# Two transformer blocks with a mixture of experts: token rows and gated products stored plainly and picked by TensorE with a stride, accumulators zeroed by GpSimd

## What is computed

```python
# per layer l, tokens t [512 in layer 0, 256 in layer 1, 1024]
g = softmax(t @ w_group + b_group); group = argmax(g)       # 4 groups of 8
e = logits inside that group; top 2 experts, shares by softmax
y[token] = sum over its 2 experts of share * ((silu(t @ w1[e]) * (t @ w3[e])) @ w2[e])
x = x + gate * y                                            # w1, w3: 1024x512, w2: 512x1024
```

## Time and profile before

| | |
|---|---|
| Median of 3 runs | 2652.04 us (2651.12 to 2653.01) |
| Profiled execution | 2647.32 us, its span 2645.5 us |
| TensorE products busy | 91% of the span |
| TensorE weight loads busy | 48% |
| VectorE, ScalarE, GpSimd busy | 32%, 15%, 3% |
| Experts of layer 0 | about 464 to 970 us of the span |
| Experts of layer 1 | about 1281 to 1760 us |

### The profile page before, as it was taken

One profiled execution on the slowest core, in us unless ns is written; L12 is line 12 of the kernel. 1 busy time (PEld: TensorE's weight loads), 2 busy tenths in 40 slices (PEclk: granted clock), 3 DMA queues, 4 the chain that ended last, 5 costly groups with the idle time before them and its releaser, 6 DMA issues.

```text
span 2645.5 us, 27917 instructions
## 1 busy us (share of the span) xinstructions
PE 2396.6 (91%) x10390; PEld 1277.5 (48%) x10390; DVE 854.1 (32%) x1691; ACT 398.0 (15%) x964; POOL 87.5 (3%) x113
## 2 busy tenths in 40 slices
PE   5888997999999979997899999978979999779998
PEld 3435546333333334444544444434748644566843
DVE  2446514333333345453322222234621002371101
ACT  1004312101000111042101110111410001241000
POOL 0110001000000001100000000000000000000000
PEclk8888897999999989998899999999989999899999
DMA  7456333999999961203599999963214442403442
GB/s 287 159 182 271 130 125 132 380 422 422 421 421 421 421 259 64 80 16 119 226 421 422 422 422 422 422 264 116 75 64 146 157 151 87 159 1 127 159 143 72
DMA packets 148931, 609.34 MB, mean 230 GB/s; under 512 B 9584, under 2 KB 19824, under 8 KB 99568
## 3 DMA queue, kind: packets, MB, share of 16 engines
q1 hardware_dynamic: 145072, 592.94, 57.3%
q10 hardware_dynamic: 2480, 10.10, 0.9%
q0 software_dynamic: 1296, 5.17, 0.5%
HBM read 594.02 MB, written 14.16 MB: 230 GB/s over the span
## 4 chain that ended last, share of the span: by engine, by line
PE 76%; DVE 10%; DMA 7%; issue 3%; ACT 2%; POOL 1%; SPq 1%; another core or an unknown queue 0%; DVEq 0%; ACTq 0%; POOLq 0%
PE psum L2188 16%; PE psum L1828 11%; PE psum L2380 8%; PE psum L2393 8%; PE psum L2201 7%; PE psum L2248 6%; PE psum L1763 3%; PE psum L2298 3%; DMA rows<-in_w 3%; DMA ring<-in_w 2%; PE psum L1820 2%; PE psum L2162 1%; POOL rstd L403 1%; PE psum L2338 1%; PE psum L1952 1%
## 5 line engine op out<-in xcount | busy, mean ns | idle before, releaser
L1828 PE MATMUL psum<-ring,hT 128*128 128x512 f32 x832 | 375.0, 610 | 13.7 <-issue 6.5
L2188 PE MATMUL psum<-ring,arena 128*64 128x512 f32 x1536 | 346.1, 598 | 5.9 <-ACT arena L758 3.7
L1828 PEld LDWEIGHTS psum<-ring,hT 128*128 128x128 f32 x832 | 160.4, 196 | 213.0 <-issue 204.7
L1441 DVE TENSOR_TENSOR arena<-arena,psum 128x512 f32<-128x512 f32 x204 | 140.2, 687 | 292.7 <-PE psum L2201 290.6
L2188 PEld LDWEIGHTS psum<-ring,arena 128*64 128x64 f32 x1536 | 112.8, 137 | 232.5 <-issue 226.8
L2393 PE MATMUL psum<-ring,arena 128*128 128x512 f32 x512 | 220.3, 592 | 3.2 <-DVE arena L1657 3.2
L2380 PE MATMUL psum<-hT,ring 128*128 128x256 f32 x1024 | 221.5, 379 | 1.3 <-DVE hT L1522 1.3
L2380 PEld LDWEIGHTS psum<-hT,ring 128*128 128x128 f32 x1024 | 194.4, 190 | 28.0 <-DVE hT L1522 1.7
L2201 PE MATMUL psum<-arena 128*128 128x512 f32 x408 | 184.2, 601 | 1.7 <-DVE arena L1504 1.7
L2248 PE MATMUL psum<-ring,arena 128*64 128x512 f32 x768 | 171.9, 596 | 7.1 <-DVE arena L1492 7.1
L2393 PEld LDWEIGHTS psum<-ring,arena 128*128 128x128 f32 x512 | 97.1, 190 | 125.5 <-issue 121.5
(11 more groups left out here) (281 smaller groups left out, 2196.6 us busy)
## 6 DMA issues: line engine op xcount, KB each, us to landing
ring<-in_w SPq DMA_DIRECT2D x288, 1024.0 KB, 10.7
rows<-in_w SPq DMA_DIRECT2D x96, 1024.0 KB, 11.9
ring<-in_w_ff SPq DMA_DIRECT2D x64, 1024.0 KB, 5.2
ring<-in_w_mod SPq DMA_DIRECT2D x48, 1024.0 KB, 11.5
ring<-in_w_in_c SPq DMA_DIRECT2D x12, 1024.0 KB, 6.3
ring<-in_w_in SPq DMA_DIRECT2D x12, 1024.0 KB, 8.1
x_rows<-arena ACTq DMA_DIRECT2D x1, 8704.0 KB, 32.0
hT<-x_rows SPq DMA_DIRECT2D x16, 512.0 KB, 14.7
```

What stands on the lines that cost most here:

```text
L1441: dve.tensor_tensor(f, f, bank, ALU.add).then_inc(v_free, 1)
L1828: inst = pe.matmul(bank, hT[:, k, P * m:P * m + P], w[k], start=k == 0, stop=k == KB - 1)
L2188: inst = pe.matmul(out[64 * e:64 * e + 64, :], xgT[:, b, k, 64 * e:64 * e + 64], m, start=k == 0, stop=k == KB - 1)
```

## The change

Token rows and gated products are written plainly. TensorE, where it reads them as the stationary operand, picks every eighth column (`hrow`, and the rows fetched from DRAM) or every fourth (`act_`). The zeroing of the three regions moves from the start of VectorE's `moe` to GpSimd: for layer 0 behind the wait for the attention's last result (`ab_out` 8), for layer 1 behind `c_out` 16, both ahead of the inverse square root of the norm before the experts. VectorE waits for it after `choose`.

```diff
-        act_by_quarter = act_.rearrange("p (f q) -> p q f", f=4)
+        act_by_quarter = act_.rearrange("p (q f) -> p f q", f=4)
+        hrow_by_eighth = hrow.rearrange("p t (q k) -> p t k q", k=KB)
...
+            def clear(nt):
+
+                pool.memset(shareT[:, 0:nt, :], 0.0)
+                pool.memset(ySlot, 0.0)
+                pool.memset(facc[:, 0:nt, :], 0.0).then_inc(cleared, 1)
...
             rsqrt_rows(4)
             rsqrt_heads(12, HD)
+            pool.wait_ge(ab_out, 8)
+            clear(4)
             rsqrt_rows(4)
             dispatch()
             pads()
             rsqrt_heads(2 * 2 + 2 * 4, HD)
             rsqrt_heads(2, P)
+            pool.wait_ge(c_out, 16)
+            clear(2)
             rsqrt_rows(2)
...
-                        act.activation(hrow[:, tile, :].rearrange("p (k q) -> p q k", k=KB)[:, 64 * h:64 * h + 64, :],
-                                       bank.rearrange("p (q k) -> p q k", k=KB), ACT.Copy).then_inc(a_free, 1)
+                        act.activation(hrow[:, tile, 512 * h:512 * h + 512], bank, ACT.Copy).then_inc(a_free, 1)
...
-                dve.memset(shareT[:, 0:nt, :], 0.0)
-                dve.memset(ySlot, 0.0)
-                dve.memset(facc[:, 0:nt, :], 0.0).then_inc(v_step, 1)
-                dve.wait_ge(v_step, so_far(v_step))
                 scalers(nt)
                 norm(2 * l + 1, 1, tiles)
                 choose(l, nt)
+                dve.wait_ge(cleared, l + 1)
...
-                        dve.tensor_tensor(act_by_quarter, quarters(bank), quarters(siluG), ALU.mult).then_inc(v_free, 1)
+                        dve.tensor_tensor(act_, bank, siluG, ALU.mult).then_inc(v_free, 1)
...
-                            inst = pe.matmul(psum[:, 5 + h, P * k:P * k + P], hrow[:, m, P * kk:P * kk + P], pick[:, b, m, :],
+                            inst = pe.matmul(psum[:, 5 + h, P * k:P * k + P], hrow_by_eighth[:, m, kk, :], pick[:, b, m, :],
...
-                            inst = transpose(psum[:, 5 + h, P * k:P * k + P], x_slots[b][:, P * kk:P * kk + P])
+                            inst = transpose(psum[:, 5 + h, P * k:P * k + P], x_slots[b].rearrange("p (q k) -> p k q", k=KB)[:, kk, :])
...
-                            inst = transpose(bank[:, P * f:P * f + P], act_[:, P * f:P * f + P])
+                            inst = transpose(bank[:, P * f:P * f + P], act_by_quarter[:, f, :])
```

More of the change, by code:

```diff
@@ L299, in build @@
         final_in, c_in = sem("final_in"), sem("c_in")
-        blanked, x_zeroed, x_placed, x_scattered, x_turned = (sem(n) for n in ("blanked", "x_zeroed", "x_placed", "x_scattered", "x_turned"))
+        cleared, blanked, x_zeroed, x_placed, x_scattered, x_turned = (sem(n) for n in ("cleared", "blanked", "x_zeroed", "x_placed", "x_scattered", "x_turned"))
         x_fetched = [sem(f"x_fetched{b}") for b in range(2)]
@@ L319, in rows_of @@
             return w.rearrange("o (p k) n -> p (o k) n", k=k)[:, at:at + n, :]
-        def quarters(x):
-            return x.rearrange("p (q f) -> p q f", f=4)
         def rows256(w, c):
@@ L1387, in late_rows @@
                             dve.wait_ge(s["a"], silu.next(2))
-                            dve.tensor_tensor(act_by_quarter, quarters(psum[:, 1, :]), quarters(siluG), ALU.mult).then_inc(s["v"], 1)
+                            dve.tensor_tensor(act_, psum[:, 1, :], siluG, ALU.mult).then_inc(s["v"], 1)
                             dve.wait_ge(s["v"], so_far(s["v"]))
@@ L2087, in late_products @@
                                 for m in range(nt):
-                                    pe.matmul(psum[:, 5 + k // 4, P * (k % 4):P * (k % 4) + P], hrow[:, m, P * k:P * k + P], pick[:, 0, m, :],
+                                    pe.matmul(psum[:, 5 + k // 4, P * (k % 4):P * (k % 4) + P], hrow_by_eighth[:, m, k, :], pick[:, 0, m, :],
                                               start=m == 0, stop=m == nt - 1)
@@ L2100, in late_products @@
                             for f in range(4):
-                                inst = transpose(psum[:, 2, P * f:P * f + P], act_[:, P * f:P * f + P])
+                                inst = transpose(psum[:, 2, P * f:P * f + P], act_by_quarter[:, f, :])
                             inst.then_inc(s["product"], 1)
```

## The result

The changed kernel takes 2703.97 us (median of 4, 2703.7 to 2704.45) against 2651.58 us before: ratio 1.0198, 95% interval 1.0176 to 1.022, 52 us slower. Its profiled execution took 2704.01 us with a span of 2702.2 us, 56.7 us more than that of before (2645.5).

A forecast was written before the change was run, and what follows sets the result against it. TensorE holds 76% of the chain, with DMA at its rate of 421 to 422 GB/s in both expert stages. -4.9 - 2.2 + 57.5 + 15 + 2.3 = +67.7 us on 2652.0 gives 2720 us; range 2640 to 2745.

The forecast's parts named there:

- rival A: TensorE's loads: strided ones cost nothing, so the kernel gets faster, -7.8 us to 2644 us; chance 0.32.
- the forecast's own part: Whole kernel: range 2700 to 2745 us around the forecast of 2720; chance 0.58, rival C included.
- B: TensorE's strided loads: half the extra cost, 0.165 us a load, +18 us to 2670; chance 0.10 with its neighbours.
- Part 1: Before the scalers: zeroing moved to GpSimd lets them begin 3.5 and 1.4 us sooner, gain 4.9 us.
- rival C: Full price in the gathers, gains lost to GpSimd's zeroing: +7, 2727 us; chance within the forecast's 0.58.
- Part 2: Layer 0's token-row evictions by ScalarE: plain writes end VectorE's wait at L1325 until the count products, gain 2.2 us.
- Part 3: Gated product 0.37 us shorter: hidden in layer 1; layer 0 could give 5.9 us, but DMA allows only 0.7.
- Part 4: TensorE's strided loads at 0.225 us, not 0.116: layer 1 +57.5, layer 0's pairs +15, first gathers +2.3 us.

The follow-up runs named there:

- DMA relieved: Kernel before, zeroing on GpSimd, layer 0 loading half of each w2 chunk: ratio 0.9968 as control, 0.9954 with the gated product also plain.
- the kernel with the rows back: Changed kernel with token rows written and read as before in both layers, zeroing on GpSimd and plain gated product kept: 2639.25 us, ratio 0.996.
- rows by layer: Changed kernel with layer 1's token rows written and read as before, layer 0's still plain and read with a step: 2645.63 us, ratio 0.999.

## Why the prediction was right, and where its terms were off

The forecast was +67.7 us, the runs gave +52.4. Direction, mechanism and place were right: the price of the strided gathers in layer 1, the change of the bound there from DMA to TensorE, pairs of 33.27 us where 33.2 were forecast, and +59.3 us for the loop where 57.5 were. That the pair came out to 0.1 us is partly luck: the forecast counted 36 loads at 0.11 us extra, but the four of the transposes pay next to nothing and the 32 of the gather pay 0.127 each, 4.07 us. The stated range, from 2640 us, held rival A as well, so to lie in it says little; the forecast's own part began at 2700, and 2704 is near its lower end. Rival A fell with the first load of the gather (0.243 instead of 0.116), B with it.

Part 1 (zeroing) was right to 0.1 us at the scalers. GpSimd hid it, and rival C did not happen.

Part 2 (evictions) was priced at 2.2 us and gave 0.3. ScalarE's evictions do take 0.60 us and the wait at L1325 went. But the end of the count products, the next wait, was read off, 1.10 us for the last eight; in the profile after they take 1.89, and so they do in every other execution on record. The granted clock was 0.93 over 443 to 447 us in the kernel before and 0.55 over 442 to 447 in the changed one, so near its higher level in the one and near its lower one in the other. The way from the router's result to the place numbers took 13.1 us in the three kernels with plain evictions and a slow router product, and 13.4 in the six with spread ones; with a fast router product it took 14.0 with plain and 13.8 to 13.9 with spread ones, the kernel before (13.4) apart. So the spread evictions cost 0.3 us at most. The step that failed is to take the end of the next wait from one execution at its clock.

Part 3 (gated product) was right in its limit: DMA's rate decides. Layer 0's loop went from 498.4 to 496.7 us, but that can't be credited to the gated product: with the token rows alone the loop took 497.4, with the gated product alone 500.7, and in four executions with an unchanged loop 497.5 to 498.9. A gain of the 0.7 us that was forecast can't be told from that spread. With DMA relieved 4.4 us came out, not 5.9: the row transposes then stand in the chain in the gated product's place, so 0.28 of the 0.37 us a pair are to be had.

Part 4 in layer 0 is the term that was wrong: +15 us for transposes that were taken to load like products. They load in 0.12 us, and the seam did not grow. The prediction used one price for "a load", taken from VectorE's reads. That transposes and products might differ was not considered, though the rows of before show that a transpose is one instruction and an fp32 product two. Without this term the forecast would have been +52.7, but so near a hit would have been luck: the terms that are left missed by 1.8 (layer 1), 3.0 (first gathers) and 1.9 us (evictions), and the two profiled executions differ by 56.7.

The first gathers were priced at +2.3 and cost 5.3 against the profile of before, 6.7 in layer 0 alone against the kernel with the rows back. The 0.20 us a load of the stretch at a granted clock of 0.61 is not what layer 0 pays: its 64 plain products followed each other in 8.8 to 10.0 us in all ten executions that have them, 0.14 to 0.16 each. And the profile of before makes the price look smaller than it is: there ScalarE's eviction starts 1.9 us after the last product of the first gather, behind a piece of the chain called "another core or an unknown queue". In the other executions it starts 0.1 us after it, in one 0.6, and that piece is in none of them; its cause is open.

The chances do not add up either: with 0.32 for rival A, of which a part was to fall within no change, "faster" can't have 0.33.

The rule of the Trainium skill (Advanced Engine Details and Errata, SBUF Cachelines), that two accesses to a line are needed for full speed, is borne out for the loads of TensorE's fp32 products: 16 took 1.97 us at two elements a line, 2.87 at 1.33, 3.6 to 3.9 at one; the moving operand was tried at one a line only, 3.9. The rule of the Trainium skill's page TensorE: Matmul & The Clock Gate, section LDWEIGHTS, that a load costs its columns alone, does not hold for these loads: 128 columns took 0.243 us with the step and 0.116 without.

The kernel that beats both is the kernel before with the zeroing moved, 0.9966 (0.9952 to 0.9979). The plain gated product on top adds nothing that these runs can tell (0.996, 0.9941 to 0.9978).

## What to carry to other kernels

A permutation put into the write of an engine that waits anyway may be cheaper than one in TensorE's read: here the extra time of 12 slow evictions, 5.4 us of ScalarE's work, almost all hidden, was traded for 608 slower loads in TensorE's gathers. Before strides are given to TensorE, count the elements per 16 bytes and look at what the loads stand beside: short fp32 products pay in full, products of 512 columns hide it, transposes pay next to nothing. These are the three cases that were run, all in fp32. And where DMA runs at its rate, a stage has no gain to give beyond DMA's lead, even when the chain shows not one wait for DMA: compare the GB/s of the stage with that of a stage in which TensorE does wait for DMA, here 421. And before a wait is priced from a trace, look at the granted clock under the instruction that would become the next wait.

## What the runs showed of the hardware

A strided fp32 load for a product takes 0.243 us, 1.9 ns an element, near VectorE's 1.79 and 1.76. It doesn't follow TensorE's clock: 16 took 3.88 us at a granted clock of 1.00, 32 products in a row took 7.89 us at 0.81 (0.247 each), and the 64 of layer 0 took 15.5 us both in the changed kernel and in rows by layer, at 0.88 and 0.83 over 449 to 465 us. Plain ones take 0.116 at full clock and 0.20 at 0.61.

A strided load for an fp32 transpose takes 0.12 us, about 0.95 ns an element, half of the product's. Why it is half no run shows.

The router product of layer 0 (64 instructions) took 9.9 to 10.1 us in five of the fourteen profiled executions and 12.6 to 12.9 in nine, over kernels with and without each part of the change, and after the same output product. The granted clock of the stretch goes with it: 0.70 over 425 to 436 us of the kernel before (10.14 us), 0.57 over 420 to 434 of the changed kernel (12.73), both between TensorE's two levels of 1.2 and 2.4 GHz. The 64 products of the plain first gather behind it took 8.8 to 9.1 us where the router product was slow and 9.9 to 10.0 where it was fast; with the strided gather they took 15.5 in all four executions, whatever the clock. Single stages next to such a change of clock can't be compared between two profiles to better than 3 us.
